# Residual sums through a PSUM bank, a weight split moved ahead of four evacuations, and two output tiles begun under the attention heads

## What is computed

```python
y = jnp.concatenate([y_conv, y_rwkv], axis=-1) @ w_out[i]
x = x + rms_norm(y, g[1])                                   # first join
y = memory_cross_attention(rms_norm(x, g[2]), mem_n, wq[i], wkv[i], wo[i])
x = x + rms_norm(y, g[3])                                   # second join
y = swiglu(rms_norm(x, g[4]), w_gu[i], w_down[i])
x = x + rms_norm(y, g[5])
```

## Time and profile before

| | |
|---|---|
| median of 3 runs | 1794.6 us (1794.26, 1794.6, 1799.52) |
| profiled execution | 1800.14 us, its span 1798.0 us |
| TensorE matmuls | busy 1678.5 us, 93% of the span |
| VectorE, ScalarE, GpSimd | 46%, 34%, 22% of the span |
| mean granted TensorE clock | 0.955 |

### The profile page before, as it was taken

One profiled execution on the slowest core, in us unless ns is written; L12 is line 12 of the kernel. 1 busy time (PEld: TensorE's weight loads), 2 busy tenths in 40 slices (PEclk: granted clock), 3 DMA queues, 4 the chain that ended last, 5 costly groups with the idle time before them and its releaser, 6 DMA issues.

```text
span 1798.0 us, 26861 instructions
## 1 busy us (share of the span) xinstructions
PE 1678.5 (93%) x11510; PEld 1377.9 (77%) x11510; DVE 834.5 (46%) x1240; ACT 604.5 (34%) x973; POOL 402.2 (22%) x349
## 2 busy tenths in 40 slices
PE   7999999989999999998988877898989899999997
PEld 6789878767788888887776666777859878888876
DVE  3468642345333333344556887635633433233234
ACT  4234332223323232343335442324433423222222
POOL 2102111112201010132034540104203432131133
PEclk8899999999999999998999889898999999999998
DMA  6124311223222222222311100013202222222221
GB/s 213 48 71 147 136 71 47 94 71 117 84 104 87 101 90 98 93 85 90 120 49 48 47 3 2 3 49 131 81 24 71 71 94 94 94 94 94 94 76 65
DMA packets 29829, 146.03 MB, mean 81 GB/s; under 512 B 4096, under 2 KB 7440, under 8 KB 14608
## 3 DMA queue, kind: packets, MB, share of 16 engines
q1 hardware_dynamic: 29712, 144.33, 22.8%
HBM read 138.03 MB, written 6.29 MB: 80 GB/s over the span
## 4 chain that ended last, share of the span: by engine, by line
PE 77%; issue 8%; DVE 7%; POOL 5%; ACT 3%; DMA 0%; POOLq 0%; SPq 0%; DVEq 0%; ACTq 0%
PE ps L153 77%; POOL zf L165 4%; DVE zf L165 2%; DVE zf L173 2%; ACT zf L162 1%; ACT zf L159 1%; POOL tn L165 1%; DVE ps L173 1%; DVE wl L165 1%; ACT zr L162 1%; ACT wh L162 0%; PE ps L156 0%; DVE zf L2292 0%; DMA raw<-in_wstream 0%; DVE zr L173 0%
## 5 line engine op out<-in xcount | busy, mean ns | idle before, releaser
L153 PE MATMUL ps<-zr,wh 128*128 128x512 f32 (+1 forms) x3936 | 1181.6, 385 | 34.0 <-DVE wl L165 13.4
L153 PEld LDWEIGHTS ps<-zr,wh 128*128 128x128 f32 x3936 | 722.4, 192 | 197.0 <-issue 13.3
L153 PE MATMUL ps<-zr,wl 128*128 128x512 f32 (+1 forms) x1968 | 748.9, 381 | 0.0
L165 POOL TENSOR_TENSOR zf<-zf 128x512 f32<-128x512 f32 (+1 forms) x253 | 297.1, 1181 | 869.1 <-ACT zf L159 581.4
L153 PEld LDWEIGHTS ps<-zr,wl 128*128 128x128 f32 x1968 | 376.5, 191 | 77.6
L165 DVE TENSOR_TENSOR wl<-raw,wh 128x1024 fp32r<-128x1024 f32 (+1 forms) x243 | 306.2, 1300 | 231.9 <-ACT wh L162 231.9
L162 ACT ACTIVATE wh<-raw 128x1024 fp32r<-128x1024 f32 (+1 forms) x243 | 240.3, 1037 | 198.4 <-PE ps L153 196.8
L159 ACT ACTIVATE zf<-zf 128x512 f32<-128x512 f32 (+2 forms) x232 | 127.6, 560 | 411.7 <-DVE zf L165 297.2
L153 PE MATMUL ps<-zf 64*64 64x64 f32 (+6 forms) x3640 | 204.1, 248 | 34.6 <-DVE zf L165 18.6
L153 PEld LDWEIGHTS ps<-zf 64*64 64x64 f32 (+3 forms) x3640 | 162.8, 149 | 75.7 <-issue 29.7
L165 DVE TENSOR_TENSOR zf<-ps,zf 128x512 f32<-128x512 f32 (+2 forms) x133 | 84.2, 639 | 214.1 <-PE ps L153 198.3
(11 more groups left out here) (94 smaller groups left out, 720.2 us busy)
## 6 DMA issues: line engine op xcount, KB each, us to landing
raw<-in_wstream SPq DMA_DIRECT2D x117, 1024.0 KB, 4.8
zf<-in_xT SPq DMA_DIRECT2D x16, 256.0 KB, 2.8
raw<-in_wstream SPq DMA_DIRECT2D x4, 768.0 KB, 4.3
kv_scratch<-zf SPq DMA_DIRECT2D x8, 256.0 KB, 2.2
x_scratch<-zf SPq DMA_DIRECT2D x8, 256.0 KB, 2.1
zf<-x_scratch SPq DMA_DIRECT2D x8, 256.0 KB, 4.5
out<-zf SPq DMA_DIRECT2D x16, 128.0 KB, 1.7
zf<-in_cu SPq DMA_DIRECT2D x1, 1256.0 KB, 9.9
```

Source lines behind the costliest of these rows:

```text
L153: return self.raw.matmul(out_, l, x, start=start, stop=stop)
L165: return self.raw.tensor_tensor(out_, a, b, o)
```

## The change

It does three things. The residual sums: the scaled slice goes to a bank of PSUM, `xr.t`, held through the join, and VectorE adds it to F(k) for all k; GpSimd keeps only the sums of squares. `into` ends with load and split of unit u0+3, in both joins. And in `bg_att`, xo's first unit is opened at head 2: k = 0 to 3 of its two tiles come before head 2's output, k = 4 and 5 before head 3's, k = 6 and 7 and the evacuations after it; the foreground loop then does only xo's second unit.

```diff
@@ passes
         pl.take("D", stat + "0.s")
         put("spread", stat + "0")
+        if tag != "dn":
+            pl.take("D", "xr.t", stat)
@@ into
         ahead("xr", name, 1, 3, 4, 5, 6, 7, 8)
         pl.rel("D", stat + "1.s")
+        pl.rel("D", "xr.t", stat)
...
         some(1, 1, 4, 5, 6, 7)
         pl.spread(new + "1")
+        pl.load(u0 + 3)
+        pl.split(u0 + 3)
@@ bg_att
                 put("att.turn", g, mt)
                 pl.rel("M", "att.t", g, mt)
             yield
+            if g == 2:
+                n = pl.next_unit("xo")
+                for j in range(2):
+                    pl.take("D", "t.xo", j)
+            if g >= 2:
+                for k in ((0, 1, 2, 3), (4, 5))[g - 2]:
+                    put("ko", n, 0, k)
             for d in range(2):
                 pl.take("M", "att.o", g, d)
                 put("att.out", g, d)
                 pl.rel("M", "att.o", g, d)
             yield
+        for k in (6, 7):
+            put("ko", n, 0, k)
+        for j in range(2):
+            put("ev.xo", j)
+            pl.rel("D", "t.xo", j)
@@ schedule
     one_bank_set()
-    for uu in range(2):
-        n = pl.next_unit("xo")
-        for j in range(2):
-            pl.tile(n, j, 2 * uu + j)
+    n = pl.next_unit("xo")
+    for j in range(2):
+        pl.tile(n, j, 2 + j)
@@ freed
+            if k and k[0] == "xr.t":
+                return ("xr.s", k[1][0:2], 7, 1)
@@ vector: xr_a
-                y, sp = half(YS[k], h), half(ps(f"{stat}{h}.s"), 0)
+                y, sp, z = half(YS[k], h), half(ps(f"{stat}{h}.s"), 0), half(ps("xr.t", stat), k % 2)
+                if k == 0 and h == 0:
+                    e.wait_ge(freed("xr.t", stat))
                 e.wait_ge(("mm", f"{stat}{h}.s"), (f"{stat}{h}.sq", k), (tag if h or k < 4 else tag + ".0", k))
-                e.stt(y, y, vec("norm_gains_2", g + k), sp, MUL, MUL).then_inc(*e.up("xr.a", name, k, h))
-                if k % 2 == 0:
-                    e.wait_ge(("xr.a", name, k, h), ("o2.xd", k))
-                    e.tt(half(F(k), h), half(F(k), h), y, ADD).then_inc(*e.up("xr.s", name, k, h))
+                e.stt(z, y, vec("norm_gains_2", g + k), sp, MUL, MUL).then_inc(*e.up("xr.a", name, k, h))
+                e.wait_ge(("xr.a", name, k, h), ("o2.xd", k))
+                if name == "xo":
+                    e.wait_ge((f"x3.rs{h}.sq", k))
+                e.tt(half(F(k), h), z, half(F(k), h), ADD).then_inc(*e.up("xr.s", name, k, h))
@@ gpsimd: xr_a
-                if k % 2:
-                    e.wait_ge(("xr.a", name, k, h), ("o2.xd", k))
-                    if name == "xo":
-                        e.wait_ge(("xr.x", "o2", k, h), (f"x3.rs{h}.sq", k))
-                    e.tt(half(F(k), h), half(F(k), h), half(YS[k], h), ADD).then_inc(*e.up("xr.s", name, k, h))
                 add_squares(f"{XR[name][2]}{h}", k)
```

## The result

The changed kernel takes **1780.8 us** in the median of 4 runs (1779.41 to 1781.84). Four runs of the kernel before gave 1796.55 us (1794.26 to 1799.52). The ratio is 0.9911, 95% interval 0.9891 to 0.9931: 15.8 us, or 0.9%, faster. The forecast was 1782.6 us in a range of 1775 to 1789. The profiled execution took 1779.41 us, with a span of 1777.4 us and a mean granted clock of 0.961 (before: 1800.14, 1798.0 and 0.955).

What follows compares the result with a forecast made beforehand. TensorE's matmuls, 77% of the chain that ended last, were taken as the bound. Terms 3.0 - 2.4 - 2.6 + 5.6 + 2.5 + 5.9 = 12.0 us, off the median 1794.6, gave 1782.6 us, range 1775 to 1789.

Steps and rivals of the forecast that it cites:

- the likeliest case: Whole kernel: the forecast itself, 12.0 us gained from 1794.6, giving 1782.6 us; chance 0.50.
- First join: Second block's residual after the mixer, feeding wq: odd slices' adds moved to VectorE shorten TensorE's waits; 3.0 us gained.
- the same here: Residual join feeding wq: waits of 1.4 and 2.95 us bring the clock to half, costing 2.8 us.
- wq's split ahead: Before the first scores: they wait for tile 1's evacuation, 2.4 us lost, and low clock loses 2.6 us more.
- The heads: Before head 2's output: xo's matmuls fill TensorE's 3.27 us wait and avoid low clock; 5.6 us gained.
- Second join: Residual join feeding gu: k=5 1.25 us sooner, k=7's 1.22 us wait gone, low clock stays; 2.5 us gained.
- gu's split ahead: gu's first tiles: the 3.40 us wait for unit 4's weights and slow run behind it go; 5.9 us gained.
- The clock stays full: Behind three shorter waits: 2.7 us more at each, gain 15 to 20 us, time 1775 to 1779; chance 0.22.
- The profiled execution is not typical: Fast executions lack low-clock spells the change removes: up to 5.4 us not there to win, 1788 us; chance 0.20.
- PSUM operands are dearer: Both joins: scaling into PSUM and its reader cost 0.13 us more a slice, 2 us in all, 1784.6 us; chance 0.05.
- Slower: Heads: the new wait before the first scores keeps the clock low, 25 us cost at two heads, 1805 us; chance 0.03.

Runs made afterwards that it cites:

- wq-only kernel: Changed kernel with the fourth unit's load and split ahead of the evacuations only for wq, for gu behind them as before: 1788.65 us, ratio 0.9954 against the kernel before.

## Why the prediction was right, and where its terms were off

**The result** came out of the likeliest case: 1780.8 against 1782.6 us, faster, in the range. Two errors partly cancelled. The sum of 12.0 us was 3.8 too small against the 15.8 of the medians (17.1 in the stages), and the base of 1794.6, a median of three, lay 2.0 us under the later one, 1796.55.

**First join** (3.0 predicted; 5.4 in the table, 4.3 against the kernel with the old sums). The mechanism holds: VectorE reads PSUM; k=5 stands 27.44 us behind the start of the region where it stood at 30.67, 3.2 us sooner (2.95 predicted), and 2.2 more come behind it, where the k=7 waits were (1.0 + 1.18). But 1.1 of the 3.2 us are not the edit's. With the old sums k=5 stands at 29.59 (1256.80 - 1227.21). Ahead of the join, behind the 2.0 us wait for GpSimd, the kernel before ran at 0.50 for 6 us; the changed one was at 0.65 from 1240 to 1242 us and at 1.00 from 1242 to 1244. So VectorE's first scaling came 13.95 us behind the start of the region in the kernel before (1243.28) and 13.0 to 13.1 in all the others, old sums included. The edit itself brings k=5 forward by 2.15 us, 0.8 less than predicted.

The step that failed is the clock. I charged 2.8 us for "the same here", a low stretch behind the waits, as if it were new. But the kernel before already paid it: its eight sums took 1.84 us at 1253.00, where 0.95 is full speed, and the changed kernel's take 1.76 at 1248.16, one stretch in place of one stretch. It also does some good, since TensorE's work, drawn out, covers most of what it would have waited for k=5: with the bank that wait is nothing, with sums in SBUF 0.27 us. By 1255.28 four spreads take 0.61 us, which is full speed. Without the charge the sum gives 5.7, the upper end that I had written; that in turn is 1.4 more than this edit alone gives.

**wq's split ahead** (-2.4 for the wait, -2.6 for the clock; measured -2.26 and -1.9). Right in place, holder and size. The 1.9 are 4.16 - 2.26; the eight scores alone lost 3.36 - 1.89 = 1.5 of it. The -2.6 is 0.7 us too much, and, as the last section shows, a chance and no fixed price. My reading that no single wait of that size stands in the trace of the kernel before was wrong. One does, and the pair behind it took 0.70 us, which is full speed:

```profile
375.64 0.70 PE L153 MATMUL ps<-zr,wh 128*128 128x512 f32 x2 [2.86 <-DVE zr L165]
```

**The heads** (5.6; 6.0): right in place and cause. The kernel without this edit splits the gain: 4.1 us of waits, and 1.7 of clock in those executions where it falls, which the 5.6 had counted as certain. The split of xo's second unit, which I costed at nothing under the 24 matmuls, indeed cost nothing: head 2's output follows them at once.

**Second join** (2.5; 4.0 in the table, 2.5 against the kernel with the old sums). k=5 comes 1.28 us sooner, 1.25 predicted: 20.46 us behind the cut ahead of it (1391.46 - 1371.00), where it was 21.74 (1402.75 - 1381.01). The k=7 wait of 1.22 is gone. The remaining 1.5 us lie behind k=5, where the low stretch is shorter, the pair taking 0.69 and not 0.79. They need no effect of the edit: the kernel with the old sums gained the same 1.5 us over the kernel before. So the term was right, and the 4.0 of the table holds luck.

**gu's split ahead** (5.9; 5.8), with the next late thing, unit 5, at 0.32 us where 0.4 was worked out: right. The wq-only kernel confirms it with 5.9 us in the stage.

**The rivals.** *The clock stays full* put the gain at 15 to 20 us, and the stages gave 17.1, but not in its way: the clock fell behind the 2.10, 2.26 and 2.60 us waits. *The profiled execution is not typical*: true in part. Taken back one by one, the edits are worth 6.8 + 4.3 + 5.9 - 4.2 = 12.8 us in the stages, close to the 12.0 of the sum. The other 4.3 of the 17.1 are low-clock stretches that the profile of the kernel before has and those of the kernels with an edit taken back have not (1.1 and 1.5 in the joins, 1.7 at the heads). But the medians gained 15.8 and not 12.8, and the same four kernels' distances from the changed one add up to 17.2 in the medians (7.7 + 5.1 + 7.9 - 3.5), so such stretches seem to cost other executions too (the changed kernel's own noise enters that sum four times); how much of the 4.3 us is typical stays open. The 5.4 us of this rival were not lost. *PSUM operands are dearer*: refuted, 422 ns against 484 in the same place of the dataflow beside GpSimd, and 0.42 against 0.42 us where nothing collides. The 65 ns more that I had worked out from the Trainium skill (VectorE: DVE Perf Modes, TRN2 errata) do not show in either; the measurement decides. *Slower*: the low stretch behind the first scores cost 1.9 us and not half of the heads.

What I did not see before the runs: the -5.0 us of my own sum was a reason to leave wq's split alone. The kernel without it is 3.5 us faster in the medians, 2.7 by the ratios and 4.2 in the stage.

## What to carry to other kernels

Moving a step ahead in a queue in program order pays where somebody downstream waits for it, and costs where somebody waits for what it is moved past. The same two lines gained 5.8 us at gu and lost 4.2 at wq, so cost each place by itself. When VectorE and GpSimd work on SBUF side by side, first take work off the one that holds the other up (4.3 us of the joins here), then try operands in PSUM (2.5 us). To know what an edit is worth, take it back alone and compare stages with that kernel: the profile of the kernel before had 4.3 us of low clock that would otherwise have been put down to the edits. Before charging a new wait with a low-clock stretch, look whether the kernel already runs that work at low clock.

## What the runs showed of the hardware that I had not expected

The same wait does not always bring the clock down. The 2.26 us wait before the first scores was followed by eight matmuls in 3.36 us in the changed kernel, 3.00 without the heads' edit and 3.09 with the split ahead for wq alone, but by 1.97 us (1.89 is full) with the sums in SBUF:

```profile
1285.41 1.97 PE L153 MATMUL ps<-zf 128*128 128x256 f32 x8 [2.26 <-issue]
```

A wait of 3.27 us before head 2's output halved the rate for some of the matmuls in the kernel before (5.37 us), and not without the heads' edit (3.67). The wait of 2.60 us at gu's k=5 was followed by a pair of 0.69 us in the changed kernel, and by one of 0.50 with the split ahead for gu alone, where the clock fell a little later, the pair at 1390.62 taking 0.80:

```profile
1389.07 0.50 PE L153 MATMUL ps<-zr,wh 128*128 128x256 f32 x2 [2.60 <-DVE zr L173]
...
1390.62 0.80 PE L153 MATMUL ps<-zr,wh 128*128 128x256 f32 x2
```

With the old sums the clock was low ahead of the wait in the same place (there 2.42 us) and full behind it. The pair at 1393.12, ahead of the wait, took 0.63 us where 0.40 is full, and the wait covered the loss:

```profile
1393.12 0.63 PE L153 MATMUL ps<-zr,wh 128*128 128x256 f32 x2
```

Where no wait covers it, such a stretch cost 1.5 to 2 us, and the executions of one kernel spread by a few us (1782.88 to 1790.5 for the kernel without the heads' edit). I take the one for a part of the other, but no run here shows it. A term for the clock behind a wait of 2 to 3.3 us is thus a chance, not a certainty, and single profiles should not be read finer than that.
